# Expert 0's first matmuls on half an input: two-halved expert input, expert 0 ahead of TensorE's loop, first quarter of w1 freed alone

## What is computed

```python
def hier_moe(h, w_rg, b_rg, w_re, b_re, w1, w3, w2):
    # top-1 of 4 groups, then top-2 of its 8 experts: 2 experts per token, 32 in all
    ...
    a = jnp.einsum('td,edf->tef', t, w1)      # w1, w3: (32, 2048, 512)
    b = jnp.einsum('td,edf->tef', t, w3)
    hid = jax.nn.silu(a) * b * cw[:, :, None]
    return jnp.einsum('tef,efd->td', hid, w2) # w2: (32, 512, 2048)
```

## Time and profile before

| | us |
|---|---|
| median of 3 executions | 1504.9 (1504.88, 1504.9, 1507.95) |
| the profiled execution | 1503.4 |
| its span, first to last instruction | 1501.5 |
| TensorE busy in the span | 1248.5 |
| VectorE busy | 736.4 |
| ScalarE busy | 209.1 |
| HBM read | 579.29 MB |

### The profile page before, as it was taken

How to read it: one execution, slowest core, us unless ns; L and a number is a source line. 1 busy time by engine, 2 the same in 40 slices (tenths; PEclk the granted TensorE clock), 3 DMA queues, 4 the chain that set the end, 5 groups by cost and what they waited for, 6 DMA issues and landing times.

```text
span 1501.5 us, 18725 instructions
## 1 busy us (share of the span) xinstructions
PE 1248.5 (83%) x7365; PEld 553.1 (37%) x7366; DVE 736.4 (49%) x976; ACT 209.1 (14%) x480; POOL 43.8 (3%) x68
## 2 busy tenths in 40 slices
PE   4799999999999998967677677776776779999967
PEld 4688544744444443322122222222221223333312
DVE  6776157877675736534224323332342244555525
ACT  3011131221111132100000000000000001111103
POOL 1001200000000001000000000000000000000010
PEclk9899999999999999998888988988898899999989
DMA  9999978888788998999999999999999999999996
GB/s 356 393 383 383 345 274 341 308 327 323 271 304 330 360 368 363 425 424 426 428 426 424 427 428 426 424 428 426 425 426 428 426 424 428 427 426 424 428 425 273
DMA packets 101652, 581.93 MB, mean 388 GB/s; under 512 B 6664, under 2 KB 31520, under 8 KB 57840
## 3 DMA queue, kind: packets, MB, share of 16 engines
q1 hardware_dynamic: 98736, 572.81, 93.8%
q10 hardware_dynamic: 1664, 6.46, 1.1%
q0 software_dynamic: 1216, 2.17, 0.5%
HBM read 579.29 MB, written 2.13 MB: 387 GB/s over the span
## 4 chain that ended last, share of the span: by engine, by line
PE 39%; DMA 27%; SPq 26%; DVE 5%; issue 2%; ACT 1%; POOL 0%; ACTq 0%; DVEq 0%
DMA stream<-in_w 23%; PE ps L692 11%; SPq L537 8%; SPq L548 8%; PE ps L777 7%; SPq L531 6%; PE ps L868 5%; DMA stream<-in_w_ada 4%; PE ps L917 3%; PE ps L617 3%; SPq L474 2%; PE ps L689 1%; PE ps L835 1%; DVE wk L1003 1%; PE ps L875 1%
## 5 line engine op out<-in xcount | busy, mean ns | idle before, releaser
L868 PE MATMUL ps<-stream,wk 128*32 128x512 f32 x2304 | 317.2, 678 | 135.8 <-DMA stream<-in_w 134.1
L1281 DVE TENSOR_TENSOR acc<-ps,acc 128x2048 f32<-128x2048 f32 x37 | 84.8, 2292 | 423.8 <-PE ps L835 423.8
L917 PE MATMUL ps<-stream,cst 128*32 128x512 f32 x1152 | 153.8, 662 | 64.5 <-DMA stream<-in_w 64.5
L868 PEld LDWEIGHTS ps<-stream,wk 128*32 128x32 f32 x2304 | 69.7, 117 | 372.5 <-issue 221.0
L692 PE MATMUL ps<-stream 128*128 128x512 f32 x448 | 197.5, 594 | 0.3 <-PE ps L617 0.3
L692 PEld LDWEIGHTS ps<-stream 128*128 128x128 f32 x448 | 83.3, 190 | 99.2 <-issue 98.5
L617 PE MATMUL ps<-stream 128*128 128x256 f32 x512 | 117.1, 392 | 2.2 <-ACT stream L1417 2.2
L777 PE MATMUL ps<-stream 128*128 128x512 f32 x256 | 112.6, 601 | 3.1 <-ACT stream L1527 1.8
L617 PEld LDWEIGHTS ps<-stream 128*128 128x128 f32 x512 | 100.3, 197 | 16.7 <-issue 2.2
L875 PEld LDWEIGHTS ps<-cst,wk 128*128 128x128 f32 x576 | 69.9, 191 | 62.0 <-issue 62.0
L835 PE MATMUL ps<-wk,cst 32*128 32x512 f32 x592 | 88.2, 667 | 0.8 <-ACT wk L1576 0.8
(11 more groups left out here) (271 smaller groups left out, 922.8 us busy)
## 6 DMA issues: line engine op xcount, KB each, us to landing
stream<-in_w SPq DMA_DIRECT2D x191, 2048.0 KB, 40.5
stream<-in_w_ada SPq DMA_DIRECT2D x64, 1024.0 KB, 5.5
stream<-in_w_in SPq DMA_DIRECT2D x8, 4096.0 KB, 16.7
stream<-in_w_ada SPq DMA_DIRECT2D x64, 384.0 KB, 10.0
stream<-in_w_out SPq DMA_DIRECT2D x4, 4096.0 KB, 15.4
stream<-in_w_ada SPq DMA_DIRECT2D x16, 512.0 KB, 9.7
stream<-in_w_in SPq DMA_DIRECT2D x4, 2048.0 KB, 14.1
stream<-in_w_in SPq DMA_DIRECT2D x2, 3072.0 KB, 16.2
```

Source lines behind the costliest of these rows:

```text
L868: last = nc.tensor.matmul(bank(1 + m)[32 * g:32 * g + 32, :], xe[:, k + g, :], w13[m][:, k + g, :], start=(k == 0), stop=(k == KD - 4))
L917: last = nc.tensor.matmul(bank(2)[32 * g:32 * g + 32, :], hid[:, k, :], w2v[:, k, 512 * g:512 * g + 512], start=(k == 0), stop=(k == 3))
L1281: V.tensor_tensor(y4, ps[:, b0:b0 + 4, :], y4, ALU.add).then_inc(ysum_sb, 1)
```

## The change

1. **Expert input in two halves.** `pick_rows` takes blocks g, g+4, g+8, g+12 for group g (rather than 4g to 4g+3), so that the first half of the 512 columns holds blocks 0 to 7. VectorE copies `xp` in two halves, TensorE transposes two blocks at a time (`turn_rows(h)`, into banks 3 and 4), and VectorE multiplies and adds each half by itself. `rows_sb`, `xe_ps`, `xe_t` and `xe_sb` rise twice a tile. The first two `up` calls wait for the first half, the other two for the second. In the loop, `turn_rows(0)` comes ahead of the transposes of `gated`, and `turn_rows(1)` behind.
2. **Expert 0 out of the loop.** TensorE's expert 0 stands ahead of the group loop, which runs over experts 1 to 30; expert 31 stands behind. The tile count of expert 0 is loaded once, as `first_hi`, after `pick_rows` and ahead of `turn_rows`; expert 0 loads nothing itself.
3. **First quarter of w1 by itself.** `a_half` rises after `up(0, 0)` and after `up(0, 4)`, and once ahead of all tiles. SP issues the first half of w2 of expert 1 as two loads of 1 MB: the first when `up(0, 0)` of expert 0's last tile is done, the other when `up(0, 4)` is. For all other experts the wait stands for the same point as before. The first load raises `unit_in[1]`, on which TensorE waits ahead of w2.

```diff
--- before.py
+++ after.py
@@ -540,7 +540,15 @@
                 done = sp.value_load(cums[0:1, bass.ds(e, 1)], min_val=1, max_val=MAX_TILES)
                 src = w2[bass.ds(e, 1)].rearrange("e p k n -> (e p) k n")
                 for j in range(2):
-                    sp.wait_ge(a_ps if j else a_half, done)
+                    if j:
+                        sp.wait_ge(a_ps, done)
+                    else:
+                        sp.wait_ge(a_half, 2 * done if isinstance(e, int) and e == 1 else 2 * done + 1)
+                    if not j and isinstance(e, int) and e == 1:
+                        sp.dma_start(half(ring(r), 0)[:, 0:D], src[:, 0, :]).then_inc(unit_in[1], 16)
+                        sp.wait_ge(a_half, 2 * done + 1)
+                        sp.dma_start(half(ring(r), 0)[:, D:2 * D], src[:, 1, :]).then_inc(ring_in[r % RING][0], 16)
+                        continue
                     if j and last:
                         for k, landing in ((2, ring_in[r % RING][1]), (3, unit_in[1])):
                             sp.dma_start(half(ring(r), 1)[:, D * (k - 2):D * (k - 1)], src[:, k, :]).then_inc(landing, 16)
@@ -808,7 +816,8 @@
             def keep_clock(n):
 
                 for _ in range(n):
-                    nc.tensor.matmul(bank(7), ident, rows(0)[:, 0:4, :], start=True, stop=True)
+                    last = nc.tensor.matmul(bank(7), ident, rows(0)[:, 0:4, :], start=True, stop=True)
+                return last
 
             pe.wait_ge(x1_row, 1)
             keep_clock(4)
@@ -819,14 +828,14 @@
             nc.tensor.matmul(rk[:, 1, :], ones, R("M")[:, 0, :], start=False, stop=True)
             pe.wait_ge(m_sb, 2)
             nc.tensor.matmul(rk[:, 2, :], ones, R("M")[:, 2, :], start=True, stop=True).then_inc(rank_ps, 1)
-            keep_clock(3)
+            keep_clock(3).then_inc(a_half, 1)
 
 
             def pick_rows():
 
                 for t2 in range(TT):
                     for g in range(4):
-                        last = nc.tensor.matmul(bank(0)[32 * g:32 * g + 32, :], pick[:, t2, :], rows(t2)[:, 4 * g:4 * g + 4, :], start=(t2 == 0), stop=(t2 == TT - 1))
+                        last = nc.tensor.matmul(bank(0)[32 * g:32 * g + 32, :], pick[:, t2, :], rows(t2)[:, g:KD:4, :], start=(t2 == 0), stop=(t2 == TT - 1))
                 last.then_inc(rows_ps, 1)
 
             def add_part(t2, b0, onto=False):
@@ -835,18 +844,21 @@
                     last = nc.tensor.matmul(ps[:, b0 + g, :], spread[32 * g:32 * g + 32, t2, :], ye[32 * g:32 * g + 32, :], start=not onto, stop=True)
                 last.then_inc(part_ps, 1)
 
-            def turn_rows():
-
-                for j in range(4):
-                    last = nc.tensor.transpose(bank(3, 4, P)[:, j, :], xp[:, P * j:P * j + P], ident)
+            def turn_rows(h):
+
+                for j in range(2):
+                    last = nc.tensor.transpose(bank(3 + h, 2, P)[:, j, :], xp[:, P * (2 * h + j):P * (2 * h + j) + P], ident)
                 last.then_inc(xe_ps, 1)
 
             pe.wait_ge(x1_row, TT)
             pe.wait_ge(pick_sb, 1)
             pick_rows()
-            pe.wait_ge(rows_sb, 1)
-            turn_rows()
             pe.wait_ge(route_sb, 1)
+            first_hi = pe.value_load(cums[0:1, 1:2], min_val=1, max_val=MAX_TILES)
+            for h in range(2):
+                pe.wait_ge(rows_sb, h + 1)
+                turn_rows(h)
+
             def expert(i, b, final=False):
 
                 e = RING * i + b
@@ -855,8 +867,11 @@
                 def landed(c):
                     return 48 * i + 16 * ((3 * b + c) // RING + 1)
 
-                lo = pe.value_load(cums[0:1, bass.ds(e, 1)], min_val=0, max_val=MAX_TILES)
-                hi = pe.value_load(cums[0:1, bass.ds(e + 1, 1)], min_val=1, max_val=MAX_TILES)
+                if b == 0:
+                    lo, hi = 0, first_hi
+                else:
+                    lo = pe.value_load(cums[0:1, bass.ds(e, 1)], min_val=0, max_val=MAX_TILES)
+                    hi = pe.value_load(cums[0:1, bass.ds(e + 1, 1)], min_val=1, max_val=MAX_TILES)
                 pe.wait_ge(ring_in[r1][0], landed(0))
                 pe.nop(nofuse=True)
                 w13 = [ring(r).rearrange("p (k f) -> p k f", k=KD) for r in (r1, r3)]
@@ -877,10 +892,11 @@
                     last.then_inc(h_ps, 1)
 
                 with pe.Fori(lo, hi) as t:
-                    pe.wait_ge(xe_sb, t + 1)
+                    pe.wait_ge(xe_sb, 2 * t + 1)
                     pe.wait_ge(spread_sb, t + 1)
-                    up(0, 0)
+                    up(0, 0).then_inc(a_half, 1)
                     up(0, 4).then_inc(a_half, 1)
+                    pe.wait_ge(xe_sb, 2 * t + 2)
                     pe.wait_ge(ring_in[r1][1], landed(0))
                     up(0, 8)
                     up(0, 12).then_inc(a_ps, 1)
@@ -901,33 +917,37 @@
                     pick_rows()
                     pe.wait_ge(ab_sb, 2 * t + 2)
                     fold_quarters(1)
-                    pe.wait_ge(rows_sb, t + 2)
+                    pe.wait_ge(rows_sb, 2 * t + 3)
+                    turn_rows(0)
+                    pe.wait_ge(rows_sb, 2 * t + 4)
                     pe.wait_ge(gated_sb, t + 1)
                     for t2 in range(TT):
                         last = nc.tensor.transpose(bank(0, 4, P)[:, t2, :], wrf[:, 320 + P * t2:320 + P * t2 + P], ident)
                     last.then_inc(spread_ps, 1)
-                    turn_rows()
+                    turn_rows(1)
                     pe.wait_ge(hid_sb, t + 1)
                     for k in range(4):
                         if k % 2 == 0:
                             pe.wait_ge(ring_in[r2][k // 2], landed(2))
+                        if k == 0 and b == 1:
+                            pe.wait_ge(unit_in[1], 16 * 7)
                         if k == 3 and final:
-                            pe.wait_ge(unit_in[1], 16 * 7)
+                            pe.wait_ge(unit_in[1], 16 * 8)
                         for g in range(4):
                             last = nc.tensor.matmul(bank(2)[32 * g:32 * g + 32, :], hid[:, k, :], w2v[:, k, 512 * g:512 * g + 512],
                                                     start=(k == 0), stop=(k == 3))
                     last.then_inc(ye_ps, 1)
 
 
-            with pe.Fori(0, NE // RING) as i:
+            expert(0, 0)
+            with pe.Fori(0, (NE - 2) // RING) as i:
                 for b in range(RING):
-                    expert(i, b)
-            for b in range(NE % RING):
-                expert(NE // RING, b, b == NE % RING - 1)
+                    expert(i, b + 1)
+            expert((NE - 2) // RING, 1, True)
 
             total = pe.value_load(cums[0:1, NE:NE + 1], min_val=NE, max_val=MAX_TILES)
             pe.wait_ge(spread_sb, total + 1)
-            pe.wait_ge(xe_sb, total + 1)
+            pe.wait_ge(xe_sb, 2 * total + 2)
             pe.wait_ge(ysum_sb, 2 * total + 2)
             pe.nop(nofuse=True)
 
@@ -1280,13 +1300,18 @@
                 y4 = ysum[t2].rearrange("p (g n) -> p g n", g=4)
                 V.tensor_tensor(y4, ps[:, b0:b0 + 4, :], y4, ALU.add).then_inc(ysum_sb, 1)
 
-            def by_column(m):
-
-                return mod[:, m, :].rearrange("p (g j) -> p j g", g=4).unsqueeze(3).to_broadcast((P, 4, 4, ROWS))
-
-            xe4 = xe.rearrange("p (g j) r -> p j g r", g=4)
-            xe_ps4 = bank(3, 4, P).rearrange("p j (g r) -> p j g r", g=4)
-
+            def by_column(m, h):
+
+                return mod[:, m, 8 * h:8 * h + 8].unsqueeze(2).to_broadcast((P, 8, ROWS))
+
+            def copy_rows(h):
+                V.tensor_copy(xp[:, S * h:S * h + S], bank(0)[:, S * h:S * h + S]).then_inc(rows_sb, 1)
+
+            def scaled(h):
+                return V.tensor_tensor(xe[:, 8 * h:8 * h + 8, :], bank(3 + h, 8, ROWS), by_column(4, h), ALU.mult)
+
+            def shifted(h):
+                return V.tensor_tensor(xe[:, 8 * h:8 * h + 8, :], xe[:, 8 * h:8 * h + 8, :], by_column(3, h), ALU.add)
 
             link(picks())
             link(both())
@@ -1296,11 +1321,13 @@
             dve.nop(nofuse=True).then_inc(route_sb, 1)
             V.memset(spread, 0.0).then_inc(spread_sb, 1)
             dve.wait_ge(rows_ps, 1)
-            V.tensor_copy(xp, bank(0)).then_inc(rows_sb, 1)
-            dve.wait_ge(xe_ps, 1)
-            V.tensor_tensor(xe4, xe_ps4, by_column(4), ALU.mult).then_inc(xe_t, 1)
-            dve.wait_ge(xe_t, 1)
-            V.tensor_tensor(xe4, xe4, by_column(3), ALU.add).then_inc(xe_sb, 1)
+            for h in range(2):
+                copy_rows(h)
+            for h in range(2):
+                dve.wait_ge(xe_ps, h + 1)
+                scaled(h).then_inc(xe_t, 1)
+                dve.wait_ge(xe_t, h + 1)
+                shifted(h).then_inc(xe_sb, 1)
             dve.wait_ge(route_sb, 1)
             total = dve.value_load(cums[0:1, NE:NE + 1], min_val=NE, max_val=MAX_TILES)
             with dve.Fori(0, total) as t:
@@ -1327,14 +1354,16 @@
```

(12 more changed lines are left out.)

## The result

The changed kernel takes 1516.31 us in the median (1513.82 to 1518.87, five runs), where the kernel before took 1504.88 to 1507.95 beside it: a ratio of 1.0068, with a 95% interval of 1.0053 to 1.0084. A fifth execution of the kernel before took 1656.0 us; it is a slow run and stands in none of these numbers. I had forecast 1503.2 in a range of 1501.2 to 1506.2. The profiled execution is 1516.31 with a span of 1514.5, 13.0 us more than before.

The account below looks back on a forecast made before the run. From about 600 us the weight stream's bytes were taken to set the end. The first load 1.93 us earlier, less 0.2 for a dry queue, gave 1.7 us: 1504.9 to 1503.2 us, range 1501.2 to 1506.2.

Parts of the forecast that it names:

- Part 2: Expert 0 out of the loop: same instructions, only two register loads gone before the first matmul; new single load costed at 0.
- my five rivals: Dry queue (0.17), register load holding the transposes (0.12), ramp gone too (0.12), fixed cost per load (0.06), TensorE's sequencer (0.06).
- The slower one: At the seam before the first expert matmul, TensorE's sequencer becomes the bound: 1507.3 us; chance 0.06.
- What an engine does inside a tile moves nothing as long as the queue doesn't run dry: Expert stage from about 600 us: bytes set the end, so only an earlier weight stream moves it.
- a rate other than 426 GB/s between 700 and 1400 us: Expert stage: a rate differing from 426 in this stretch was named as a sign that the prediction is wrong.
- The chain to the first matmul: From `pick_rows` to the first `up`: halved input starts TensorE at 579.78 instead of 580.80, 1.02 us earlier.
- the early count: Before the first expert matmul: two register loads (1.0 us) would be late by 0.5 us; loading one count early avoids it.
- The first load: SP's first load of w2 after the hole: issued at 580.84 instead of 582.77, 1.93 us earlier.
- The dry queue at 592 us: At the next request, margin falls from 3.1 to 2.3 us; charged 0.2 us, bounds 0 and 0.9.
- the rival that the quarter adds nothing: Around 592 us, the dry queue takes all that TensorE's chain doesn't give: 1503.9 us; chance 0.17.
- The fixed cost of a second load: At the split w2 load, the second quarter pays its own ramp of 1.7 us: 1504.9 us, no change; chance 0.06.
- The tail isn't touched: Behind the last w2 quarter: same instructions, 19 us from there to the end, no change.

Follow-up runs that it names:

- run 8: Changed kernel with 96 semaphore-raising instructions spread over three idle places on TensorE's queue ahead of the loop: 0.9992 of the kernel before.
- run 3: Changed kernel with expert 0 back in the group loop, loading its own two counts; halves and quarter kept: 1.0004 of the kernel before.
- run 10: Changed kernel with 96 semaphore-raising instructions, without the quarter (expert 1's first half of w2 as one 2 MB load): 0.9994 of the kernel before.
- run 1: Kernel before with 62 empty instructions that don't reach the chip, so the kernel before once more: 0.9992.
- run 11: Kernel before with 120 semaphore-raising instructions in three idle places ahead of the loop: 1504.19 us beside 1505.91 of the kernel before, executed once.
- run 12: Kernel before with 150 semaphore-raising instructions in three idle places ahead of the loop: 1506.27 us beside 1505.91 of the kernel before, executed once.
- run 14: Kernel before with 105 semaphore-raising instructions in three idle places ahead of the loop: 1516.83 us beside a median of 1505.27, executed once.
- run 15: Changed kernel without the quarter, with 48 semaphore-raising instructions (24 and 24) ahead of the loop: 1.0072 of the kernel before.
- run 2: Changed kernel with 100 empty instructions that don't reach the chip, so the changed kernel once more: 1.0048 of the kernel before.
- run 4: Kernel before with only expert 0 taken out of the loop and its count loaded early: 1.0024 of the kernel before.
- run 5: Kernel before with 62 semaphore-raising instructions behind TensorE's first transpose: 1.0021 of the kernel before.
- run 6: Changed kernel with 100 semaphore-raising instructions behind TensorE's first transpose: 1.0016 of the kernel before.
- run 7: Changed kernel with 194 semaphore-raising instructions behind TensorE's first transpose: 1.0103 of the kernel before.
- run 9: Kernel before with 74 semaphore-raising instructions (32 and 42) in two idle places ahead of the loop: 1.0054 of the kernel before.
- run 13: Kernel before with 90 semaphore-raising instructions in three idle places ahead of the loop: 1517.94 us beside a median of 1505.27, executed once.

## Why the prediction was wrong, point by point

**The step that failed** is in Part 2: "The instructions that expert 0 issues are the same", costed at nothing for all but the register loads. The instructions are the same, but with the peeling 318 more instructions stand ahead of the loop, and these moved the loop to where each return fetches it anew. I had the row from which one could be warned, and did not read it: the instruction queue's 24 packets are fewer than six passes over a loop of over six packets would need, so the loop was being kept. No one of my five rivals was this. The slower one put TensorE's sequencer at the seam, 1507.3 us, and none of the five stalls is there.

The Trainium skill has the rule, "Runtime: NRT & Kernel Launch", section on the mechanics of instruction fetch: TensorE keeps 128 KiB of instructions, 2048, refilled in blocks of 256, and a taken branch whose target isn't in the current window of two blocks waits for a fetch. The runs agree in kind (packets of 16 KB, long stalls only at the return). They don't agree with a window of two blocks, since the loop of the kernel before is over six blocks long and was kept; and a loop of 1607 instructions, well under 2048, already missed.

**"What an engine does inside a tile moves nothing as long as the queue doesn't run dry"** held only in part. The five waits are 31 us in sum, the stream lost 9.5 (910.8 against the 901.3 of run 8, which has all of the change). I can place 8.8 of it. Between 640 and 1480 us the mean rate is 423.0 GB/s instead of 426.0 in run 8: 3.0 x 840 / 426 = 5.9 us. The 45 packets more carry 0.74 MB: 0.74 / 0.427 = 1.7 us. And in the last 14 us ahead of the last quarter and the 3 behind it, 0.52 MB less goes through, 1.2 us, as if the DMA engines no longer finished together. Which engines bring the instructions I didn't look at, so the cause of that last term is argued, not shown. The prediction had named a rate other than 426 GB/s between 700 and 1400 us as a sign that it is wrong, and it is 422 (columns as in the earlier trace rows):

```profile
700.00:1400.00 700.00, 529.62 (x3998) 178.77 (x3994) 267.22 (x478) 65.60 (x134) 0.00 (x0) 0.89 1.00 422
```

Most of the 5.9 us lies where the queue did run dry. SP's loads around the last stall:

```profile
1325.74 3.12 SPq L537 DMA_DIRECT2D stream<-in_w  x2
1353.38 2.24 SPq L556 DMA_DIRECT2D stream<-in_w  x2
1362.12 0.87 SPq L531 DMA_DIRECT2D stream<-in_w  x2
1368.96 1.25 SPq L537 DMA_DIRECT2D stream<-in_w  x2
1387.96 2.23 SPq L556 DMA_DIRECT2D stream<-in_w  x2
```

The stall of 6.6 us ends at 1332.29 at an expert with two tiles, and the next two-tile expert follows soon. In this stretch TensorE, not the stream, sets the pace: the chain that ended last runs through TensorE alone from 1256 to 1438 us. A part of it (start, length, what):

```profile
1308.41 3.43 PE ps L883 x32
...
1325.68 6.61 issue
1332.29 5.46 PE ps L883 x32
...
1351.61 3.43 PE ps L883 x32
```

The stop costs more than its 6.6 us. The matmuls right behind it take 5.46 us where the same ones take 3.43 at the other tiles, and the granted clock between 1330 and 1335 us is 0.50, that is 1.2 GHz:

```profile
1330.00:1335.00 5.00, 2.71 (x16) 0.76 (x18) 0.00 (x0) 0.00 (x0) 0.00 (x0) 0.50 1.01 419
```

From 1353.38 on only two more requests go out before 1387.96, and three windows later show the price:

```profile
1380.00:1385.00 5.00, 5.00 (x50) 2.34 (x43) 3.95 (x12) 0.39 (x1) 0.00 (x0) 1.00 0.94 397
1385.00:1390.00 5.00, 5.00 (x48) 1.48 (x44) 0.45 (x2) 0.92 (x2) 0.00 (x0) 1.00 0.59 229
1390.00:1395.00 5.00, 5.00 (x44) 1.86 (x40) 3.36 (x3) 0.56 (x2) 0.00 (x0) 1.00 0.94 378
```

(427 - 397 + 427 - 229 + 427 - 378) x 5 / 427 = 3.2 us in these alone. The first four stalls, with a full queue behind them, cost far less.

**The chain to the first matmul** was right: 1.16 us earlier (forecast 1.02), a half's operation took 0.42 us (0.43), and the early count is worth its place (run 3). There I had expected 0.5 us to remain of the halves' gain without it. Nothing remained: two register loads and the loop's entry came to 1.22 us where the prediction has 0.5.

**The first load** was right too, 2.01 us earlier (1.93), and the next request came 14.52 us behind `pick_rows` (14.66 forecast, 15.68 before).

**The dry queue at 592 us** was right as a mechanism and mis-sized as a term: 0.2 us forecast, 0.7 in the mean of six runs and up to 1.3. I had chosen the value near the favourable bound against the row that spoke for the other: 2.3 us of margin where a request takes 3.2 to full rate. The end of the stream gave back some 1 us more, which the prediction has nowhere. So the rival that the quarter adds nothing (0.17) is what run 10 shows. Of the 1.7 us forecast, run 8 has 0.6 from `pick_rows` to the last quarter (906.40 against 906.98).

**The fixed cost of a second load** didn't show: the second quarter's load went out 0.86 us behind the first, and the rate was 217 GB/s from 584 to 586 us and 410 and 426 in the two windows behind, so no second ramp shows. The figure that the prediction quotes beside this rival stands in a section on loads that GpSimd issues, and these are SyncE's.

**"The tail isn't touched"** was wrong by 1.3 us in this execution, by the granted clock and not by the instructions. The changed kernel behind the last quarter, and its window (columns as in the earlier trace rows):

```profile
1494.32 1.06 PE L937 MATMUL ps<-stream,cst 128*32 128x512 f32 x8 [1.38 <-DMA stream<-in_w]
...
1496.20 2.09 PE L844 MATMUL ps<-wk,cst 32*128 32x512 f32 x8 [0.81 <-ACT wk L1605]
```

```profile
1495.00:1500.00 5.00, 4.19 (x15) 1.53 (x12) 1.50 (x1) 2.08 (x3) 0.00 (x0) 0.66 0.04 16
```

The addition of the last part takes 2.09 us instead of 1.14, at a mean granted clock of 0.66: TensorE is at 1.2 GHz for some 3 us. Before that it had been idle for 1.38 us, at work for 1.06 and idle again for 0.81; but the kernel before, with 1.41, 1.06 and 0.81, kept the full clock there. Runs 1, 3, 11, 12, 14 and 15 have the short tail (18.8 to 18.9 us), runs 2 and 4 to 10 the long one (20.2 to 20.3), run 13 has 21.7, and it goes with neither the place of the loop nor any part of the change. What decides it is open.

## What to carry to other kernels

An instruction that costs nothing where it stands can cost time where others then come to stand: compare the packets of the instruction queue before and after any edit that adds code ahead of a long loop, and look for waits on "issue" at the loop's return. If a kernel lives from a stream, a stall elsewhere is free only while requests are outstanding; find the stretch with the smallest reserve first. And when a first request is moved up, the second has to move with it, or part of the gain is lost as a dip one request later.

The change is worth keeping only with the loop put right. Then it, with the quarter (0.9992) or without (0.9994), is at best 0.1% faster than before, and neither interval excludes no change.

## What the runs showed of the hardware

- TensorE's instructions come in packets of 16 KB. A loop of 1607 to 1619 instructions was kept over all its passes at some places and fetched anew at others, nine packets a pass. Starts at 60 to 110 places of 256 behind that of the kernel before were bad, 0, 1, 120 and 150 to 162 good, and none between 1 and 60 was tried.
- A miss at the return stops TensorE for 4.8 to 7.1 us. The next packet comes another 3.5 to 3.9 us later (runs 9 and 13), and where the loop starts just ahead of a packet's edge both waits are one of 10.1 to 11.7 us (runs 14 and 15).
- After the last such stop, of 6.6 us, TensorE ran at 1.2 GHz, and 32 matmul records took 5.46 us instead of 3.43.
- An instruction that does nothing but raise a semaphore took 0.15 us on TensorE's queue, and one that neither waits nor signals doesn't reach the chip at all.
